# Gate units of a 1-core kernel in 512-column matmuls, half by half into whole banks, and the angle tables behind the second slab's split

## What is computed

```python
proj = xn @ w_in[l]
(q, k, v, qi, ki, wi, sc_u, sc_b, sc_c, rw_z, gate_pre) = jnp.split(proj, split_points, axis=-1)
...
up = jnp.einsum('bsgc,gcd->bsgd', branches, w_branch[l])
gates = jax.nn.sigmoid(gate_pre + b_gate[l]).reshape(bsz, seq, N_BRANCH, D_MODEL)
mixed = jnp.sum(gates * up, axis=2)
h = h + mixed @ w_out[l]
```

## Time and profile before

| | us |
|---|---|
| three runs | 1671.14, 1671.31, 1672.34 (median 1671.31) |
| the profiled execution | 1671.93 |
| its span, first to last instruction | 1670.1 |
| PE busy in the span | 1658.8 (99%) |
| VectorE busy | 1197.7 (72%) |
| ScalarE busy | 964.4 (58%) |
| GpSimd busy | 211.6 (13%) |
| mean granted clock of TensorE | 0.998 |

### The profile page before, as it was taken

One profiled execution on the slowest core, in us unless ns is written; L12 is line 12 of the kernel. 1 busy time (PEld: TensorE's weight loads), 2 busy tenths in 40 slices (PEclk: granted clock), 3 DMA queues, 4 the chain that ended last, 5 costly groups with the idle time before them and its releaser, 6 DMA issues.

```text
span 1670.1 us, 29758 instructions
## 1 busy us (share of the span) xinstructions
PE 1658.8 (99%) x12384; PEld 1477.8 (88%) x12384; DVE 1197.7 (72%) x1676; ACT 964.4 (58%) x1459; POOL 211.6 (13%) x208
## 2 busy tenths in 40 slices
PE   9999999999999999999999999999999999999998
PEld 6999999999998999999999998778788987788887
DVE  7877447798888975548888875767756647677564
ACT  6674425565567565345555564666774556657743
POOL 1764400000002945100000000000000100000000
PEclk9999999999999999999999999999999999999999
DMA  7443523454545424425454545435345453443451
GB/s 265 150 152 117 181 102 119 185 201 177 185 163 196 158 102 158 146 98 184 156 204 176 185 187 179 150 127 176 134 172 178 180 195 130 149 173 130 168 185 51
DMA packets 48197, 268.17 MB, mean 161 GB/s; under 512 B 13568, under 2 KB 14464, under 8 KB 16448
## 3 DMA queue, kind: packets, MB, share of 16 engines
q1 hardware_dynamic: 38160, 263.65, 43.9%
q10 hardware_dynamic: 9136, 1.58, 0.5%
q0 software_dynamic: 768, 1.05, 0.2%
HBM read 264.42 MB, written 1.84 MB: 159 GB/s over the span
## 4 chain that ended last, share of the span: by engine, by line
PE 96%; DVE 2%; ACT 1%; issue 0%; DMA 0%; DVEq 0%; SPq 0%; ACTq 0%
PE bank L1490 13%; PE bank L1491 12%; PE bank L1492 12%; PE bank L2649 11%; PE bank L2651 10%; PE bank L2650 10%; PE bank L1543 8%; PE bank L1545 4%; PE bank L2679 2%; PE bank L1939 1%; PE bank L2667 1%; PE bank L1778 1%; PE bank L2711 1%; PE bank L1780 1%; PE bank L1779 1%; PE bank L1983 1%
## 5 line engine op out<-in xcount | busy, mean ns | idle before, releaser
L969 DVE TENSOR_TENSOR w_low<-slab,w_high 128x2048 fp32r<-128x2048 f32 x249 | 580.4, 2340 | 204.5 <-ACT w_high L596 197.5
L596 ACT ACTIVATE w_high<-slab 128x2048 fp32r<-128x2048 f32 x249 | 470.2, 1896 | 114.8 <-PE bank L2651 71.8
L1490 PE MATMUL bank<-act,w_high 128*128 128x256 f32 (+1 forms) x1744 | 502.0, 288 | 0.9 <-DVE w_low L969 0.9
L1491 PE MATMUL bank<-act,w_high 128*128 128x256 f32 (+1 forms) x1744 | 493.2, 283 | 0.0
L1492 PE MATMUL bank<-act,w_low 128*128 128x256 f32 (+1 forms) x1744 | 493.1, 283 | 0.0
L1490 PEld LDWEIGHTS bank<-act,w_high 128*128 128x128 f32 (+1 forms) x1744 | 332.8, 191 | 11.0 <-issue 5.6
L1491 PEld LDWEIGHTS bank<-act,w_high 128*128 128x128 f32 (+1 forms) x1744 | 333.1, 191 | 0.9 <-issue 0.5
L1492 PEld LDWEIGHTS bank<-act,w_low 128*128 128x128 f32 (+1 forms) x1744 | 333.0, 191 | 0.1
L2649 PE MATMUL bank<-w_high,act 128*128 128x512 f32 x768 | 305.7, 398 | 0.0
L2651 PE MATMUL bank<-w_low,act 128*128 128x512 f32 x768 | 299.8, 390 | 0.0
L2650 PE MATMUL bank<-w_high,act 128*128 128x512 f32 x768 | 299.2, 390 | 0.0
(11 more groups left out here) (261 smaller groups left out, 1856.6 us busy)
## 6 DMA issues: line engine op xcount, KB each, us to landing
slab<-stream_a SPq DMA_DIRECT2D x143, 1024.0 KB, 4.8
slab<-stream_b SPq DMA_DIRECT2D x104, 1024.0 KB, 4.8
residual<-x_t SPq DMA_DIRECT2D x4, 256.0 KB, 6.2
slab<-stream_a ACTq DMA_DIRECT2D x2, 512.0 KB, 5.8
lora_weights<-lora SPq DMA_DIRECT2D x2, 512.0 KB, 7.7
out_t<-residual SPq DMA_DIRECT2D x4, 256.0 KB, 2.3
d_inverse<-arena POOLq DMA_DIRECT2D x2, 256.0 KB, 3.8
constants<-common SPq DMA_DIRECT2D x1, 384.0 KB, 9.1
```

The source lines that it names most:

```text
L596: line.did(eng.activation(core.wh[u % PARTS][:, 0:SLAB_WIDTH[u]], core.slab[u % SLABS][:, 0:SLAB_WIDTH[u]], ACT.Copy), core.sem("slab_high"))
L969: line.did(line.eng.tensor_tensor(core.wl[u % PARTS][:, 0:SLAB_WIDTH[u]], core.slab[u % SLABS][:, 0:SLAB_WIDTH[u]], core.wh[u % PARTS][:, ...
L1490: eng.matmul(out, wh, xh, start=first, stop=False, skip_group_check=True)
L1491: eng.matmul(out, wh, xl, start=False, stop=False, skip_group_check=True)
```

## The change

Three things.

1. **Gate units become wide.** Each half unit (128 rows) is 8 pairs of a 512-column and a 256-column matmul (`wide_product`, as for up) into a bank of its own, by the new `gate_half`. A gate unit so takes two banks and two fills; the reader is VectorE. The rotation over banks 0 to 2 goes on, and becomes ga0 (0, 1), ga1 (2, 0), ga2 (1, 2), ga3 (0, 1), gb0 (2, 0), gb1 (1, 2), gb2 (0, 1), gb3 (2, 0), br0 (1, 2) and (0, 1), br1 (2, 0) and (1, 2), gc0 (0, 1), gc1 (2, 0), gc2 (1, 2), gc3 (0, 1), br2_0 (2, 0); from br2 on it is as before.
2. **Emptying a gate.** ScalarE copies the right half of each bank (two copies a unit), VectorE adds it to the left half into the gate's tile (two additions a unit) and tells `gate_summed`; ScalarE makes the two sigmoids in place one unit later, and for the last unit of each group of four also those of its own unit at once, for which it waits for VectorE's additions.
3. **Angles.** "angles" 1 and 2 move behind the split of w1's slab and the four squares.

```diff
--- before.py
+++ after.py
@@ -47,6 +47,7 @@
            + [("br0", i) for i in range(2)] + [("br1", i) for i in range(2)]
            + [("gc", i) for i in range(4)] + [("br2", i) for i in range(2)]
            + [("out", i) for i in range(4)])
+GATES = ("ga", "gb", "gc")
 LAG_DOWN = 2
 NARROW_UP = 4
 
@@ -143,6 +144,7 @@
 
 
 ARENA = 81
+REST_G_ = (43, 80)
 IDLE_ = 2
 
 Z_, GA_, GB_ = 0, 14, 22
@@ -247,9 +249,9 @@
 
     rows, product, fill, freed, banks = [], 0, 0, {}, []
     for kind, i in units:
-        fills = 2 - 2 * i if kind in ("q", "w") else 2 if kind.startswith("br") else 0 if kind == "down" else 1
+        fills = 2 - 2 * i if kind in ("q", "w") else 2 if kind.startswith("br") or kind in GATES else 0 if kind == "down" else 1
         parts = 1 if kind == "up" else 1 + i if kind in ("q", "w") else 4 if (kind, i) == ("down", FT // 2 - 1) else max(fills, 1)
-        reader = "act" if kind in ("rz", "ga", "gb", "gc") else "dve"
+        reader = "act" if kind == "rz" else "dve"
         first = product
         banks = []
         if kind == "up" and i >= NARROW_UP:
...
@@ -360,8 +362,8 @@
         steps = [("angles", 0)]
         for n in range(2):
             steps += [("scaled", n), ("round_half", n), ("split_half", n)]
-        return (steps + [("angles", 1), ("angles", 2)] + halves[1] + [("round", 1), ("split", 1)]
-                + [("square", i) for i in range(4)] + [("root_table", 0), ("gather", 0)])
+        return (steps + halves[1] + [("round", 1), ("split", 1)] + [("square", i) for i in range(4)]
+                + [("angles", 1), ("angles", 2), ("root_table", 0), ("gather", 0)])
     steps = []
     for n in range(2):
         steps += [("add", 2 * n), ("add", 2 * n + 1)] + halves[n] + [("square", 2 * n), ("square", 2 * n + 1)]
@@ -665,6 +667,11 @@
     return core.ar[:, RAW_ * T:RAW_ * T + 4 * (T + 1)].rearrange("p (r j t) -> p r j t", r=2, j=2)
 
 
+def gate_tile(core, n, k):
+
+    return flat(core, (GA_ if n < 4 else GB_) + 2 * (n % 4) + k)
+
+
 def scalar_a(core, eng, line, stage):
     rows, sem, bank, vec, layer = PLAN_A, core.sem, core.bank, core.vec, int(stage[1])
 
@@ -760,15 +767,18 @@
         elif kind == "cb":
             emptied(core, eng, rows, u)
             act(core.xh[:, 4 + 2 * i:6 + 2 * i, :], core.a(CONV_ + 2 * i, 2), ACT.Copy, sem("yb_high"))
-        elif kind in ("ga", "gb", "gc"):
-            made(core, eng, rows, u)
-            g = "abc".index(kind[1])
-            if kind == "gc":
-                eng.wait_ge(*sem("summed").upto(4))
+        elif kind in GATES:
+            n = 4 * GATES.index(kind) + i
             for k in range(2):
-                act(flat(core, (GA_ if g == 0 else GB_) + 2 * i + k), bank[banks[0][0]][:, k * T:k * T + T],
-                    ACT.Sigmoid, sem(f"act_emptied{banks[0][0]}") if k else None,
-                    bias=vec[:, VA["b_gate"] + 8 * g + 2 * i + k:][:, 0:1])
+                made(core, eng, rows, u, k)
+                if n:
+                    eng.wait_ge(*sem("gate_summed").upto(2 * n - 1 + k))
+                act(flat(core, REST_G_[k]), bank[banks[k][0]][:, T:2 * T], ACT.Copy, sem("rest_copied"))
+            for n in [n - 1] * (i > 0) + [n] * (i == 3):
+                eng.wait_ge(*sem("gate_summed").upto(2 * n + 2))
+                for k in range(2):
+                    act(gate_tile(core, n, k), gate_tile(core, n, k), ACT.Sigmoid, sem("gates"),
+                        bias=vec[:, VA["b_gate"] + 2 * n + k:][:, 0:1])
         elif kind == "br2":
             for k in range(i, 2):
                 mixed_high(2 * i + k)
@@ -1183,13 +1193,21 @@
             did(tt(flat(core, CONV_ + 2 * i, 2), bank[banks[0][0]][:], flat(core, CONV_ + 2 * i, 2), ALU.mult),
                 sem(f"dve_emptied{banks[0][0]}"))
             low(4 + 2 * i, 2, core.a(CONV_ + 2 * i, 2), "yb_high", "yb_ready")
+        elif kind in GATES:
+            n = 4 * GATES.index(kind) + i
+            for k in range(2):
+                b = banks[k][0]
+                eng.wait_ge(*sem("rest_copied").next(eng))
+                line.settled()
+                did(tt(gate_tile(core, n, k), bank[b][:, 0:T], flat(core, REST_G_[k]), ALU.add), sem(f"dve_emptied{b}"))
+                line.tell(sem("gate_summed"))
         elif kind in ("br0", "br1", "br2"):
             g = int(kind[2])
             for k in range(2):
                 at = 4 * i + 2 * k
                 src = flat(core, (GA_ if g == 0 else GB_) + at, 2)
                 if i == 0 and k == 0:
-                    emptied(core, eng, rows, UA["g" + "abc"[g], 3])
+                    eng.wait_ge(*sem("gates").upto(8 * g + 8))
                 made(core, eng, rows, u, k)
                 did(tt(src, bank[banks[k][0]][:], src, ALU.mult), sem(f"dve_emptied{banks[k][0]}"))
                 if g:
@@ -1536,10 +1554,10 @@
         b = rows[u][4][0][0]
         return b, {0: 1, 2: 7}[b]
 
-    def wide_product(u, j, k):
+    def wide_product(u, out, j, k):
 
         wh, wl = (w[(first + u) % PARTS][:].rearrange("p (k j m) -> p k j m", k=8, j=2) for w in (core.wh, core.wl))
-        at, out = inputs["up"](rows[u][1], k), core.bank[up_banks(u)[j]]
+        at = inputs[rows[u][0]](rows[u][1], k)
         eng.matmul(out[:].rearrange("p (n t) -> p n t", n=2), wh[:, k, j, :], core.x[:, :, at, :], start=k == 0, stop=False,
                    skip_group_check=True)
         return eng.matmul(out[:, 0:T], wl[:, k, j, :], core.xh[:, at, :], start=False, stop=k == 7, skip_group_check=True)
@@ -1553,7 +1571,7 @@
         banks.held[partner] = banks.held[b]
         for j in range(2):
             for k in range(8):
-                last = wide_product(u, j, k)
+                last = wide_product(u, core.bank[(b, partner)[j]], j, k)
         last.then_inc(sem("products").sem, 1)
 
     def down(u):
@@ -1583,8 +1601,20 @@
                 if k == nk - 1 and j % 2:
                     last.then_inc(sem("products").sem, 1)
 
+    def gate_half(u, part):
+
+        if part == 0:
+            eng.wait_ge(sem("slab_split").sem, first + u + 1)
+        b, reader, _ = rows[u][4][part]
+        banks.fill(b, reader)
+        for k in range(8):
+            last = wide_product(u, core.bank[b], part, k)
+        last.then_inc(sem("products").sem, 1)
+
     def half(u, part):
         kind, i, _, _, fills = rows[u]
+        if kind in GATES:
+            return gate_half(u, part)
         branch = kind.startswith("br")
         bank, reader, _ = fills[part if branch else 0]
         if part == 0:
```

More of the change, by code:

```diff
@@ L316 @@
 RAISED = {"a": dict(
-    act_emptied0=6, act_emptied1=7, act_emptied2=6, act_emptied3=11, act_emptied4=6, act_emptied5=8,
+    act_emptied0=2, act_emptied1=2, act_emptied2=3, act_emptied3=11, act_emptied4=6, act_emptied5=8,
     act_emptied6=11, act_emptied7=5, blend_set=1, blocks_in=16, blocks_written=128, bonus_in=1, bonus_kept=1,
     bonus_made=2, bonus_shifted=1, c_copied=4, chunk_made=8, clamped=1, columns_turned=4, conv_done=4,
-    convolved=22, decay_made=2, decays=1, diagonal=2, dve_emptied0=20, dve_emptied1=10, dve_emptied2=19,
+    convolved=22, decay_made=2, decays=1, diagonal=2, dve_emptied0=28, dve_emptied1=19, dve_emptied2=26,
@@ L321 @@
     dve_emptied3=10, dve_emptied4=6, dve_emptied5=10, dve_emptied6=8, dve_emptied7=6, exps=4, g_made=2,
[L322 to L330, removed]
@@ L331 @@
-    yb_ready=2, yc=2, yc_high=2, yc_ready=2, z_mixed=7,), "b": dict(
+    gate_input=1, gate_summed=24, gates=24, gathered=3, hidden=22, hidden_high=22, hidden_low=22,
+    index_scores=4, index_summed=4, index_weighted=8, index_weights=1, inverses_in=128, inverses_written=16,
+    k_scale=1, keys_blended=1, keys_ready=1, keys_scaled=1, ki_copied=1, ki_made=1, kk=1, kk_squared=1,
+    kk_summed=1, lora_inputs=1, lora_out=2, masked=1, maxed=4, mean_square=2, mix_high=4, mix_ready=4,
+    newest_tap=22, norm_spread=2, normed=4, off_diagonal=1, outputs_turned=2, products=96, qk_raw=6,
@@ new lines @@
+    queries_ready=1, rate_made=2, reset_made=1, rest_copied=42, rhs_made=4, rooted=1, rooted_sums=2, roped=6,
+    row_kept=1, sa_made=4, scored=4, silu=22, solved=8, spread_made=4, squared=8, state=3, state_made=3,
+    summed=8, summed_decay=2, tok_made=6, tokens_scaled=1, transposes_in=128, turned=8, u_made=3,
+    up_scaled=22, weighted=4, x_high=12, x_ready=12, y_made=4, y_rooted=1, y_scale=1, y_squared=2,
+    y_variance=1, ya_done=2, ya_high=2, yb_high=2, yb_ready=2, yc=2, yc_high=2, yc_ready=2, z_mixed=7,), "b": dict(
```

## The result

The changed kernel takes 1693.94 us (four runs, 1693.25 to 1695.49) against 1671.24 us: a ratio of 1.0135, 95% interval 1.0123 to 1.0147. The forecast was slower, 1686.9, within 1679 to 1695. The sign and four of the five places of the loss were right. The likeliest case was 7 us too low: the fall of the clock at br2_0, a case that had 0.17, came true in both layers, the wide units gave back less than forecast, and gb2 waited too.

A forecast was written before the change was run, and what follows sets the result against it. PE's stream of matmuls bounds the kernel; stalls of 9.4 us less savings of 1.6 give 7.8 a layer, 15.6 for two, angles 0: 1687.5 us profiled, 1686.9 predicted, range 1679 to 1695.

The forecast's parts named there:

- five places of the loss: PE waits forecast at ga1, post 1, solve 1, solve 2 and br2_0, 9.4 us a layer together.
- likeliest case: The whole kernel: stalls less savings make it slower, 1686.9 us; chance 0.56.
- clock case: Rival: the clock falls behind D's wait at br2_0, 2.9 to 5.8 us more a layer, 1692 to 1698; chance 0.17.
- signs of being wrong: Wait at br2_0 absent or below 3 us, C's waits absent, or a clock dip near 276 us in both layers.
- Matmuls: Gate units: wide ones save 0.1 to 0.15 us each, taken as 1.6 us a layer; four in a row 22.6.
- A: ga1's second half: bank 0 waits for the addition behind the split of ga2; PE waits 1.6 us.
- B: Post 1, bank 7: ScalarE's copy of tok 1 comes late behind blocks_out; PE waits 0.5 us.
- Additions: Each gate unit: VectorE's two additions, with the wait for its own result between them, about 1.0 us.
- Through gb, PE runs 1.65 us late: Step in C, gb units: PE 1.65 us late, less 0.6 for four wide units; no wait forecast at gb2.
- C: Solve 1 and 2: gb3's additions and sigmoids delay solve 0's copies; PE waits 2.0 us, then 0.5 more.
- D: br2_0: bank 0 waits for gc3's additions, which stand behind the split of br2_1; PE waits 4.8 us a layer.
- bound of -0.9: Angles: PE's 0.9 us earlier start of w1 carried through; the forecast took 0, as lost again at norm_x.

The follow-up runs named there:

- run with bonus_shift later: The reordered kernel with GpSimd's bonus_shift moved from ahead of its blocks_in issues to behind them: 1670.23 us, ratio 1.0000.
- reordered kernel: Three splits moved, plus the sigmoids of ga3 made behind tok 2 and those of gb3 behind solve 1: 1671.14 us, ratio 0.9996.
- aligned run with gc alone: The changed kernel with only gc wide, ga and gb narrow, the bank rotation skipping one ahead of gb1 and of gb3: 1685.06 us, ratio 1.0081.
- run with the clock held: The changed kernel with 23 unread 512-column matmuls made while PE waits for bank 0 before br2_0: 1689.77 us.
- gc3's additions ahead: The changed kernel with round and split of br2_1's slab moved behind unit gc3: 1686.63 us, ratio 1.0092.
- three splits moved: The changed kernel with gc narrow and the splits moved: ga2's behind unit ga0, ga3's behind mask 3, gb3's behind unit gb1: 1674.82 us, ratio 1.0021.
- only gc wide, rotation shifted: The changed kernel with only the four gc units wide, ga and gb narrow, bank rotation shifted by one: 1692.39 us, ratio 1.0126.

## Why the prediction was right, and where not

The measured time lies 1.1 us inside the upper end of the range, which the clock case had set; the likeliest case alone doesn't explain it. Of the prediction's own signs of being wrong one came true, the dip of the granted clock in both layers.

From norm_x on PE loses 22.5 us. Of these 19.5 are waits (18.8 forecast) and 3.8 the clock (0 in the sum), and 0.8 comes back (3.2 forecast).

- *Matmuls.* Four wide gates in a row took 23.66 us with a wait of 1.00 in it, 22.66 without, for 22.6 forecast. ga0, alone between other work, took 5.82 instead of 5.92. But of 1.6 us a layer only 0.4 came back in the first: 0.4 between gb0 and solve 2 and 0.4 between solve 2 and gc3, each beside the listed waits, while PE needed 0.4 more from ga1 to ga2, in gaps too short to be listed. Of the terms that the sum has, the saving was mis-sized most; what makes these gaps was not tried.
- *A, B.* 1.6 and 0.5 forecast, 1.44 and 0.57 measured in the first layer, 1.4 and none in the second. The earlier trace rows had nearly all of it. The changed kernel's VectorE:

```profile
143.69 3.25 DVE L979 TENSOR_TENSOR w_low<-slab,w_high 128x2048 fp32r<-128x2048 f32 x1
147.04 0.42 DVE L1202 TENSOR_TENSOR arena<-bank,arena 128x256 f32<-128x256 f32 x1
147.68 0.42 DVE L1202 TENSOR_TENSOR arena<-bank,arena 128x256 f32<-128x256 f32 x1 [0.21 <-DVE arena L1202]
```

- *Additions.* Sized 1.0 us a unit, measured 1.2: 0.42 each as forecast, but 0.64 from start to start, and 0.1 between the split's end and the first.
- *gb2.* Not forecast, 1.0 us a layer. The step that failed is "Through gb, PE runs 1.65 us late", which puts the waits inside gb at nothing and shows no working for it. The split of gb3's slab met GpSimd's two long operations and took 6.47 us:

```profile
183.37 6.47 DVE L979 TENSOR_TENSOR w_low<-slab,w_high 128x2048 fp32r<-128x2048 f32 x1 [1.38 <-ACT w_high L598]
...
183.42 2.41 POOL L2214 TENSOR_TENSOR arena<-arena,constants_a 128x1024 f32<-128x1024 f32 x1
185.78 1.90 POOL L2170 TENSOR_TENSOR arena<-arena,vectors 128x1024 f32<-128x1024 f32 x1
```

A split alone takes 2.29 us; this one took 4.2 longer, about the 2.41 + 1.90 of the two. Additions, which read a bank and one arena tile, stayed at 0.42 also beside a GpSimd operation of 2.23 us (at 143.77 in the run with bonus_shift later). In the Trainium skill, page "SBUF — State Buffer", section "SBUF: two separate sides", a VectorE instruction with two SBUF inputs and a GpSimd instruction that reads SBUF exclude each other for a whole instruction. The trace agrees. This could have been read ahead of the change: the same split was already stretched to 5.14 us by the same two operations in the kernel before, where no bank hung on it:

```profile
180.66 2.42 POOL L2184 TENSOR_TENSOR arena<-arena,constants_a 128x1024 f32<-128x1024 f32 x1
181.94 5.14 DVE L969 TENSOR_TENSOR w_low<-slab,w_high 128x2048 fp32r<-128x2048 f32 x1 [3.89 <-ACT w_high L596]
183.03 1.90 POOL L2140 TENSOR_TENSOR arena<-arena,vectors 128x1024 f32<-128x1024 f32 x1
```

- *C.* 2.5 forecast. Measured 1.8 and no second wait at solve 2 in the first layer, 1.0 in the second: over-sized; that ScalarE's backlog was smaller is my reading and was not tried by itself. That the cause is the last sigmoid's wait is shown by the reordered kernel.
- *D.* 4.8 forecast, 5.37 and 5.78 measured; the additions' 1.2 instead of 1.0, twice in that chain, is part of it. It is shown by the aligned run with gc alone, where D and the clock behind it are all there is: 13.3 us for the two layers against the kernel before in the same comparison (1671.72).
- *The clock.* My sum left it out and gave it 0.17, as a price of 2.9 to 5.8 a layer. It fell in both layers and cost 2.4 and 1.4 us by the stretches behind D, 4.2 in both by the run with the clock held. This is the largest piece of the 7 us between forecast and result. The missing saving is 2.4, gb2 2.0 and D 1.6, less 2.2 at C and 0.8 at A and B: that C was over-sized by as much as gb2 was left out is luck. The mechanism of the clock was right, its chance too low, and its price too high. It fell behind all six waits of 5.37 us and more that the traces show. By the Trainium skill's page "TensorE: Matmul & The Clock Gate", section "What's actually happening", the throttled state is the default and activity releases it. The trace agrees: 0.50 behind the wait, 1.00 again once PE had worked.
- *Angles.* 0 forecast, 0 within the measurement, which can't tell it from the bound of -0.9; norm_x came at 24.22, 24.4 forecast.

## What to carry to other kernels

Changing who empties a bank changes whose program order holds it: look at what stands ahead of the new reader's instruction in its engine's list, not at how busy the engine is. Halving what a bank holds halves the time in which it must be emptied, and the cheapest cure tried here is to move the new instruction, or the long one ahead of it, by one step; it took the loss away, but no order here is shown to gain. A new wait can cost more than its own length: count the clock behind it as a price of its own. When banks rotate, a changed number of fills moves every later user, so print the rotation before comparing variants.

## What was not expected of the hardware

The clock doesn't follow a wait's length alone. All waits of PE between 1.8 and 2.5 us in the traces, and the granted clock behind them:

| run | wait ahead of | us | lowest clock behind |
|---|---|---|---|
| the changed kernel | solve 1, first layer | 1.81 | 1.00 |
| gc3's additions ahead | solve 1, first layer | 1.81 | 1.00 |
| three splits moved | solve 1, first layer | 1.84 | 0.50 |
| gc3's additions ahead | br2_0, second layer | 1.97 | 0.50 |
| gc3's additions ahead | br2_0, first layer | 2.00 | 1.00 |
| only gc wide, rotation shifted | up 4, first layer | 2.45 | 0.50 |
| only gc wide, rotation shifted | up 4, second layer | 2.46 | 1.00 |

The windows behind the last two:

```profile
340.00:345.00 5.00, 3.97 (x14) 3.37 (x15) 4.47 (x9) 3.43 (x5) 0.00 (x0) 0.66 0.61 213
...
840.00:845.00 5.00, 5.00 (x30) 4.35 (x29) 3.62 (x5) 2.32 (x4) 0.00 (x0) 1.00 0.49 164
```

In the three of these cases in which it fell, it did so 0.6 to 0.7 us after PE had started again (at 202.5 for a start at 201.88, at 771.3 for 770.64, at 341.6 for 341.03), so a full clock during the wait says nothing of what comes. Shorter waits left it full in every trace here, but for the one of 1.07 us at the kernel's very end, with little work for PE ahead of it (0.50).
